# The order of two output-weight transfers and two expert-weight transfers on SyncE's queue

## What is computed

```python
    o = _rms(o) * norm_w.astype(F32) * jax.nn.silu(
        z.astype(F32).reshape(bsz, seq, GDN_V_HEADS, GDN_HEAD_DIM))
    return o.reshape(bsz, seq, GDN_VAL_WIDTH).astype(x.dtype) @ w_out
...
        x = _layernorm(DEEPNORM_ALPHA * x + h, ln_g[i, 0], ln_b[i, 0])
        h = _hier_moe(x, moe_w_group[i], moe_b_group[i], moe_w_router[i], moe_b_router[i],
                      moe_w_gate[i], moe_w_up[i], moe_w_down[i])
```

## Time and profile before

| | |
|---|---|
| median of three timed runs | 1015.89 us |
| the profiled execution, its own time | 1013.74 us |
| its span | 1012.4 us |
| TensorE busy | 968.9 us (96%) |
| VectorE busy | 548.3 us (54%) |
| ScalarE busy | 329.3 us (33%) |
| GpSimd busy | 52.5 us (5%) |
| DMA, mean over the span | 209 GB/s |

### The profile page before, as it was taken

How to read it: one execution, slowest core, us unless ns; L and a number is a source line. 1 busy time by engine, 2 the same in 40 slices (tenths; PEclk the granted TensorE clock), 3 DMA queues, 4 the chain that set the end, 5 groups by cost and what they waited for, 6 DMA issues and landing times.

```text
span 1012.4 us, 21876 instructions
## 1 busy us (share of the span) xinstructions
PE 968.9 (96%) x9305; PEld 757.2 (75%) x9305; DVE 548.3 (54%) x1160; ACT 329.3 (33%) x872; POOL 52.5 (5%) x81
## 2 busy tenths in 40 slices
PE   9999999999999999799867899999999999999999
PEld 6888888888888894345323588988888988877887
DVE  3875866866868334111100596875555465184675
ACT  3455456446536222001100223132121331233550
POOL 1111011011000000000000000000000000024000
PEclk9999999999999999899987999999999999999999
DMA  8213214234146998999999934442555344552221
GB/s 345 88 64 134 99 65 157 76 110 180 70 150 262 423 399 353 428 430 429 434 430 410 411 157 148 169 172 84 180 187 174 140 167 167 187 189 83 84 84 42
DMA packets 33622, 211.61 MB, mean 209 GB/s; under 512 B 4385, under 2 KB 8929, under 8 KB 15089
## 3 DMA queue, kind: packets, MB, share of 16 engines
q1 hardware_dynamic: 33520, 210.16, 53.8%
HBM read 209.03 MB, written 1.11 MB: 208 GB/s over the span
## 4 chain that ended last, share of the span: by engine, by line
PE 82%; DMA 7%; SPq 5%; DVE 3%; ACT 2%; issue 2%; POOL 0%; ACTq 0%; DVEq 0%; POOLq 0%
PE ps L552 11%; PE ps L3138 9%; PE ps L578 5%; PE ps L3038 5%; SPq L1888 4%; DMA xt<-in_wu 4%; PE ps L3809 3%; PE ps L2002 3%; PE ps L3778 3%; PE ps L3907 2%; PE ps L2647 2%; PE ps L794 2%; PE ps L958 2%; PE ps L3178 2%; PE ps L2884 2%; PE ps L600 2%
## 5 line engine op out<-in xcount | busy, mean ns | idle before, releaser
L552 PE MATMUL ps<-xt,slots 128*128 128x256 f32 x512 | 122.3, 384 | 0.0
L552 PEld LDWEIGHTS ps<-xt,slots 128*128 128x128 f32 x512 | 93.8, 190 | 12.8 <-issue 0.4
L1288 DVE SCALAR_TENSOR_TENSOR arena<-arena 128x256 f32<-128x256 f32 x128 | 56.1, 496 | 0.0
L2002 PE MATMUL ps<-arena 128*32 128x512 f32 x224 | 47.7, 635 | 6.9 <-DMA arena<-in_w 6.1
L2342 DVE TENSOR_TENSOR arena<-arena,ps 128x256 f32<-128x256 f32 x8 | 3.4, 421 | 88.8 <-ACT arena L2132 88.8
L2002 PE MATMUL ps<-slots,arena 128*32 128x512 f32 x192 | 47.5, 640 | 2.5 <-DMA xt<-in_wu 2.5
L4310 POOL TENSOR_TENSOR arena<-arena 128x512 f32<-128x512 f32 (+1 forms) x8 | 17.8, 2260 | 596.5 <-DVE arena L4118 596.5
L2132 ACT ACTIVATE arena<-ps 128x256 f32<-128x256 f32 x8 | 3.1, 385 | 114.2 <-PE ps L2002 114.2
L2002 PEld LDWEIGHTS ps<-arena 128*32 128x32 f32 x224 | 11.8, 115 | 26.7 <-issue 19.6
L3809 PE MATMUL ps<-xt,slots 128*128 128x256 f32 x128 | 30.6, 385 | 0.6 <-ACT arena L4010 0.6
L958 PE MATMUL ps<-slots,yt 128*128 128x256 f32 x128 | 28.6, 380 | 2.0 <-DMA slots<-in_wu 2.0
(11 more groups left out here) (584 smaller groups left out, 2115.9 us busy)
## 6 DMA issues: line engine op xcount, KB each, us to landing
slots<-in_wu SPq DMA_DIRECT2D x91, 1024.0 KB, 5.9
arena<-in_wu SPq DMA_DIRECT2D x20, 1024.0 KB, 14.4
arena<-in_w SPq DMA_DIRECT2D x5, 4096.0 KB, 28.9
slots<-in_w SPq DMA_DIRECT2D x8, 2048.0 KB, 34.0
extra<-in_w SPq DMA_DIRECT2D x2, 4096.0 KB, 29.4
yt<-in_w SPq DMA_DIRECT2D x3, 2048.0 KB, 30.5
extra<-in_wu SPq DMA_DIRECT2D x4, 1024.0 KB, 19.5
xt<-in_wu SPq DMA_DIRECT2D x4, 1024.0 KB, 30.7
```

The costliest lines, as they stand in the source:

```text
L552: q = M.matmul(bank(b, T), self.slots[:, s, k, n * P:(n + 1) * P], self.xt[:, k, :], start=(k == 0), stop=(k == KT - 1))
L1288: q = V.scalar_tensor_tensor(g.cn[:, s], src, w, g.cn[:, s], ALU.mult, ALU.add)
L2002: q = M.matmul(self.ps[r, 2, :], g.xg[:, half * (KT // 2) + k, r], self.flat(slots[e])[:, k * 512:(k + 1) * 512], start=(half == 0 and k = ...
```

## The change

Two lines move up in `gdn_sync` by three lines of code. Before, SP issued expert units 8 and 9 (slots 9 and 8) and then `w_out` units 5 and 7 (slots 3 and 2). After, it issues units 5 and 7 directly behind `w_out` units 1 and 3, ahead of its wait for `u_scaled(QKH)`, and expert units 8 and 9 behind them. Nothing is added or removed, and no other engine's program changes.

```diff
         self.fill(0, U_GOUT + 1)
         self.fill(1, U_GOUT + 3)
+        self.fill(3, U_GOUT + 5)
+        self.fill(2, U_GOUT + 7)
         SP.wait_ge(*g.u_scaled(QKH))
         for u in (8, 9):
             self.fill(RING[u], U_MOE + u)
-        self.fill(3, U_GOUT + 5)
-        self.fill(2, U_GOUT + 7)
         self.fill(RING[10], U_MOE + 10)
         self.fill(RING[12], U_MOE + 12)
         for s in (20, 21):
```

## The result

The changed kernel took 1022.07 us (median of 7 runs, 1015.08 to 1025.13) against 1015.89 us before: a ratio of 1.0047, 95% interval 1.0025 to 1.0069. It is slower, and outside the range of 1013.6 to 1017.1 us.

A forecast was written before the change was run, and what follows sets the result against it. The prediction took TensorE, holding 82% of the chain that ended last, as the bound. Its terms -2.04 + 1.87 + 0 gave -0.2 us, from 1015.89 to 1015.7 us, range 1013.6 to 1017.1 us.

The forecast's parts named there:

- Units 5 and 7: At L958: these w_out units land earlier in the line, so TensorE no longer waits for unit 5; -2.04 us.
- Units 8 and 9: Expert units land later, at 343.8 and 346.25 us, but are first used at 397.27 us; they cost nothing.
- Does the line run empty: Transfers near 334 to 336 us: a gap before unit 5's data, taken as 0, bounds 0 and +1.4 us.
- the start of 0.9 to 1.5 us behind the issue: In the transfer line: a new transfer's first bytes were claimed to come 0.9 to 1.5 us after its issue.
- the argument that the slow engines, which set every landing, still had work: Around unit 3's landing at 336.4 us: the 16 engines don't run empty together, so the gap was taken as 0.
- The upper bound, from the 1 MB transfer alone: Unit 5's start: 4.7 us to landing less 2.5 us of data, so 2.2 us and a gap of 1.0 us.
- The prediction's own sign for the gap: Wrong if `in_lnf` lands later than 363.5 us with DMA share under 0.9 in 334 to 336 us.
- Where the 2.04 us go: At L1928: TensorE arrives earlier but waits for router weights, as `in_lnf` still lands at 363.05 us; +1.87 us.
- The rest: From 364 us on: the transfers' restart follows TensorE, so a shift of 0.17 us passes through to the end.
- the line running empty: Rival, chance 0.17: a gap of 1.0 to 1.4 us delays `in_lnf` and L1928; net +0.8 to +1.2 us.

The follow-up runs named there:

- `after`: Trace of the changed kernel's profiled execution in the first series, the fastest of its 7 runs: 1015.08 us.
- e2: Changed kernel with expert unit 8 kept ahead of w_out units 5 and 7, only unit 9 behind them: 1015.86 us, ratio 1.0004.
- e3: Changed kernel with expert units 22 and 23 issued behind the router's five small transfers: 1014.29 us, ratio 0.9988.
- e4: Kernel before with expert units 22 and 23 issued behind the router's five small transfers: 1016.99 us, ratio 1.0009.
- e11: Changed kernel with expert unit 8 ahead of w_out units 5 and 7, and units 22 and 23 behind the router's transfers: 1013.37 us, ratio 0.9977.
- e1: The changed kernel timed and traced again, no edit: 1020.41 us (12 runs), ratio 1.0044 to the kernel before.
- e5: Changed kernel with five extra 128x256 products on TensorE ahead of its wait for the folded router weights: 1016.82 us, ratio 1.0014.
- e6: Kernel before with four scratch VectorE products ahead of the folded router weights, so TensorE idles at L1928: 1017.99 us, ratio 1.0031.
- e7: Changed kernel with `out_rest(1, 3)` moved ahead of TensorE's wait for the folded router weights: 1014.56 us, ratio 0.9983.
- e10: Kernel before with `out_rest(1, 3)` moved ahead of TensorE's wait for the folded router weights: 1016.13 us, ratio 1.0003.
- e12: e11 with `out_rest(1, 3)` also moved ahead of TensorE's wait for the folded router weights: 1012.83 us, ratio 0.9973.
- e8: Kernel before with expert unit 10 also issued ahead of w_out units 5 and 7, lengthening the L958 wait: 1020.66 us (5 runs), ratio 1.0039.
- e9: Changed kernel with `out_rest(1, 3)` moved behind the wait for the folded weights but ahead of the router product: 1018.78 us, ratio 1.0028.

## Why the prediction was wrong

- **Units 5 and 7** (-2.04 us): right. Issued at the same moments, landed 4.7 us sooner after issue, no idle time at L958.
- **Units 8 and 9** (nothing): right; nothing ever waited for them.
- **Does the line run empty** (taken as 0, bounds 0 to +1.4): the term was mis-sized. It is 0.7 us by the bytes and 0.8 by `in_lnf`. What failed in it is the start of 0.9 to 1.5 us behind the issue, where the rows of `after` show 1.8 to 2.0, and the argument that the slow engines, which set every landing, still had work. It held for units 5 to 10, which landed only 0.3 us later than in an unbroken line (unit 5 in 5.9 us instead of 5.6), and not for what came behind: unit 12 landed 0.9 us late, `in_lnf` 0.8. The upper bound, from the 1 MB transfer alone, gave a gap of 1.0 us and was the better guide. The Trainium skill (DMA: Bandwidth & Descriptors, Latency and other measured facts) has a fixed cost of some 2 us, which the prediction did not take into its sum; the size agrees with these rows, but the page puts most of it down to the receipt from the target memory, and what the rows show is a late first byte. The prediction's own sign for the gap, a DMA share under 0.9 in 334 to 336 us, was a poor one: `in_lnf` did land after 363.5 us, at 364.0, but the share was 1.29 and 0.56, 0.93 in the mean. The GB/s show the gap.
- **Where the 2.04 us go** (+1.87): right about the wait, wrong about its price, which is the next but one point. L1928 waits for `in_lnf`, and `in_lnf` lies in the line (e2: used at 363.0 us as before; e3, e4, e11: earlier with fewer bytes ahead). With the gap it is 2.52 us in `after` and 2.28 in e1; without it 1.47 in e2.
- **The rest** (passes on): in part. L1867 moved by +0.74 us, 0.22 of it the late start, and the span by +1.4; the 0.7 us that came behind L1867 are not explained by any run.
- **The step that failed: the clock was put at nothing, and it is the largest term.** The prediction moved 2 us of idle time from one place on TensorE to another and priced it as time alone: 2.04 against 1.87. In the place where it was, it cost 2 us and nothing else: none of 97 runs reached 1019 us. In its new place the clock can fall to the 1.2 GHz level behind it, for 10 us in e1, which adds 5 us there; 16 of the 19 runs of this kernel took over 1018.94 us, 13 of them at a clock of 0.983 or lower. e5 (idle time filled: no run under 0.985) and e6 (idle time made without the change: 4 of 12 runs) show that it is this and not the transfers. The trace of before had hints: behind L1928 come products of 72 and 36 columns, behind L958's wait come products of 256, and the windows of rows 6 and 10 show only stretches where the clock was 1.00, while it stood at 0.93 from 410 to 600 us.
- **The rivals.** The one that ended on the other side, the line running empty, is what the trace `after` shows: L1928 starts 0.63 us later, 0.22 of it the late start, so 0.4, where the rival gave +0.8 to +1.2 with a gap of 1.0 to 1.4 us, and its own sum with the measured gap of 0.7 to 0.8 gives 0.5 to 0.6. Its bound of +1.2 us was still far under the measured +4.6 to +6.2, which no rival had.

For the median: e5 puts the gap at +0.9 us, e1 stands at +4.6; the difference of 3.7 us is the clock's. It was worked out from medians on different chips, and three runs of e5 were over 1018.94 us without a clock under 0.985, so its size is good to about 1 us, by my estimate.

## What to carry to other kernels

An idle time that moves is not priced by its length alone: look at what TensorE does behind it, and at the granted clock there in more than one execution, since one trace can be the lucky one. Where a transfer is brought forward in a saturated line, follow what now becomes late (a 16 KB transfer with 6 MB ahead of it), and keep so many bytes ahead of a blocked issue that they last for the start of the next transfer, here one more unit. The pair of edits that takes both waits away (e11) gained 2.8 us, where the first alone lost 4.6.

## What the runs showed of the hardware

- TensorE's clock fell to the 1.2 GHz level behind an idle time of 2.28 us in e1, and not behind 2.52 us in `after`, the same kernel. It differs from execution to execution; rates are needed, not one trace. By the idle time ahead of L1928 in the trace, the runs with a mean clock of 0.983 or lower were 14 of 19 at 2.3 to 2.5 us, 4 of 12 at 1.40 us (e6), 2 of 12 at 1.47 us (e2), none of 12 at 0.35 us (e5) and 3 of 69 where nothing idles there (e3, e4, e7, e10, e11, e12); 2 of 97 in the kernel before. Where in the kernel the clock was low is known for the profiled executions only.
- How long it stayed low differed: 10 us ahead of light products (e1), 3.4 us ahead of products of 128x256 (e8, idle time 4.54 us). In e9 it fell while TensorE's rows were full (7.89 of 8 us busy, then 0.50), in products of at most 128 columns. The Trainium skill (TensorE: Matmul & The Clock Gate, Part 1) says that the clock follows how busy TensorE has been of late; e1 and e8, where it fell behind an idle time, agree, and e9 shows that it can also fall while the rows of light products read as full.
- The first bytes of a transfer that was issued into a line with some 1.1 us of work left by the sum of its bytes came too late to join it, 1.8 to 2.0 us behind the issue: 0.7 us were lost.
- Left open: what share of the low clock is due to the idle time and what to the light products (e9), where the clock was low in the runs without a trace, and why the time still spreads by some 5 us in the kernel before (1014.0 to 1018.94 us, at clocks of 0.983 to 0.990).
